# Two transformer blocks on one core: first projections among the transposes of h, and gate and up with 512 columns moving

## The reference

```python
# first block
h = rms_norm(x, mix_norm_g);  proj = h @ w_in          # queries, keys/values, gates, conv input
attn = nsa_attention(q, kv, gates, rel_bias, ...)      # compressed, selected and window branches
conv = silu(layer_norm(depthwise_conv31(a * sigmoid(g))))
x = x + concat([attn, conv]) @ w_out
h = rms_norm(x, ffn_norm_g)
u = depthwise_conv3(h @ w_up);  a, gate = split(u)      # 2 x 5632 columns
x = x + (silu(gate) * a) @ w_down;  x = rms_norm(x, final_norm_g)
# second block
ada = silu(c) @ w_ada + b_ada                           # six shift / scale / gate vectors
h = rms_norm(x, g_pre_mix) * (1 + scale_m) + shift_m;  z = h @ w_in_2
o = concat([mla_mixer(...), gla_mixer(...)]) @ w_out_2
x = x + gate_m * rms_norm(o, g_post_mix)
h = rms_norm(x, g_pre_ffn) * (1 + scale_f) + shift_f
f = (silu(h @ w_ffn_gate) * (h @ w_ffn_up)) @ w_ffn_down   # 5632 columns each
x = x + gate_f * rms_norm(f, g_post_ffn)
```

## Time and profile before

| what | value |
|---|---|
| runs | 2502.04, 2501.56, 2496.78 us; median 2501.56 |
| profiled execution | time 2500.57 us, span 2498.7 us |
| mean granted TensorE clock | 0.965 of full speed |
| busy share of the span | PE 94%, DVE 64%, ACT 44%, POOL 1% |
| HBM read | 494.31 MB |

### The profile page before, as it was taken

How to read it: one execution, slowest core, us unless ns; L and a number is a source line. 1 busy time by engine, 2 the same in 40 slices (tenths; PEclk the granted TensorE clock), 3 DMA queues, 4 the chain that set the end, 5 groups by cost and what they waited for, 6 DMA issues and landing times.

```text
span 2498.7 us, 37713 instructions
## 1 busy us (share of the span) xinstructions
PE 2359.4 (94%) x15624; PEld 2121.9 (85%) x15624; DVE 1603.2 (64%) x2266; ACT 1109.9 (44%) x1725; POOL 23.3 (1%) x59
## 2 busy tenths in 40 slices
PE   6989899899999999999979999996999999999997
PEld 5879777689998899998858787675999988999985
DVE  3996656678887778888765464646555555545444
ACT  3423566444444334444445464544434444444442
POOL 0000000000000000000000000000000000000000
PEclk9989989989999999999989899997999999999998
DMA  7745412668888888888854453252666667655552
GB/s 184 245 138 168 131 51 76 219 211 276 277 275 285 310 279 279 272 287 290 297 166 147 146 186 109 85 173 102 212 225 214 226 232 222 222 177 186 186 193 76
DMA packets 137770, 502.02 MB, mean 201 GB/s; under 512 B 15312, under 2 KB 15312, under 8 KB 137344
## 3 DMA queue, kind: packets, MB, share of 16 engines
q1 hardware_dynamic: 136368, 494.37, 58.6%
q0 software_dynamic: 1232, 5.24, 1.3%
HBM read 494.31 MB, written 5.24 MB: 200 GB/s over the span
## 4 chain that ended last, share of the span: by engine, by line
PE 84%; DVE 10%; ACT 3%; DMA 1%; issue 1%; POOL 1%; SPq 0%; ACTq 0%; DVEq 0%
PE bank L573 77%; DVE conv_y L1535 3%; DVE w_lo L1462 3%; PE bank L722 1%; DMA raw<-weights 1%; PE bank L757 1%; PE bank L545 1%; ACT w_hi L1034 1%; PE bank L610 0%; PE bank L739 0%; DVE wide L1480 0%; PE bank L622 0%; PE bank L752 0%; DVE x L1994 0%; DVE wide L1992 0%
## 5 line engine op out<-in xcount | busy, mean ns | idle before, releaser
L1462 DVE TENSOR_TENSOR w_lo<-raw,w_hi 128x1024 fp32r<-128x1024 f32 x737 | 888.0, 1220 | 550.6 <-ACT w_hi L1034 550.3
L573 PE MATMUL bank<-h_hi,w_hi 128*128 128x256 f32 x3472 | 993.7, 286 | 21.0 <-DVE w_lo L1462 20.6
L1034 ACT ACTIVATE w_hi<-raw 128x1024 fp32r<-128x1024 f32 x737 | 759.8, 1052 | 522.2 <-PE bank L573 503.4
L573 PE MATMUL bank<-h_lo,w_hi 128*128 128x256 f32 x3472 | 986.9, 284 | 0.0
L573 PE MATMUL bank<-h_hi,w_lo 128*128 128x256 f32 x3472 | 986.7, 284 | 0.0
L573 PEld LDWEIGHTS bank<-h_hi,w_hi 128*128 128x128 f32 x3472 | 670.1, 193 | 31.8 <-DVE w_lo L1462 30.9
L573 PEld LDWEIGHTS bank<-h_lo,w_hi 128*128 128x128 f32 x3472 | 670.4, 193 | 0.1
L573 PEld LDWEIGHTS bank<-h_hi,w_lo 128*128 128x128 f32 x3472 | 669.9, 193 | 0.0
L573 PE MATMUL bank<-w_hi,ff_hi 128*128 128x512 f32 x704 | 276.0, 392 | 2.9 <-DVE w_lo L1462 2.9
L573 PE MATMUL bank<-w_lo,ff_hi 128*128 128x512 f32 x704 | 274.0, 389 | 0.0
L573 PE MATMUL bank<-w_hi,ff_lo 128*128 128x512 f32 x704 | 274.0, 389 | 0.0
(11 more groups left out here) (293 smaller groups left out, 1818.1 us busy)
## 6 DMA issues: line engine op xcount, KB each, us to landing
raw<-weights SPq DMA_DIRECT2D x924, 512.0 KB, 4.4
bias_rows<-table POOLq DMA_DIRECT2D x1, 3072.0 KB, 35.5
raw<-weights SPq DMA_DIRECT2D x5, 504.0 KB, 3.4
x<-x SPq DMA_DIRECT2D x2, 1024.0 KB, 5.8
bias<-bias_rows POOLq DMA_DIRECT2D x1, 2048.0 KB, 17.1
out<-x SPq DMA_DIRECT2D x8, 256.0 KB, 2.0
lasting<-params SPq DMA_DIRECT2D x1, 550.0 KB, 7.7
raw<-weights SPq DMA_DIRECT2D x1, 488.0 KB, 3.2
```

The source lines that it names most:

```text
L573: t = e.matmul(out, s, m, start=opens and first and q == 0, stop=closes and last and q == 2)
L1034: e.activation(w_hi[:, n % PART_SLOTS, 0:widths[i]], raw[:, i % RAW_SLOTS, 0:widths[i]], ACT.Copy).then_inc(hi_ready, 1)
L1462: e.tensor_tensor(w_lo[:, slot, 0:widths[i]], raw[:, i % RAW_SLOTS, 0:widths[i]], w_hi[:, slot, 0:widths[i]].bitcast(F32), ALU.subtract).t ...
```

## The change

The first projections of a stage are issued among the transposes. `need(k)` turns up to four steps ahead, through four banks, and `project` calls it ahead of its wait for the weights. In stages 0 and 1 the first two tiles are made together (`tile_pair`), with their chunks laid out in turn; in stages 2 and 3 the first group runs so. ACT and DVE take weight chunks between their steps of h, at the steps in `WITH_H`, and DVE scales the second half of `wide` between them. The rel_bias table now comes before stage 0. In the second block's FFN gate and up are groups of 512 columns (the last of each half 256); the product has tokens on the partitions and is turned by PE in pairs of tiles (`turn_product`), after the first chunk of the next group. The ada chunks pause for the last of `out_attn` and the first pair of the first FFN, and then come at a rate of 0.6.

```diff
+FF_GROUPS = [[(6 * half + g, P * FF_HALF * half + 512 * g, min(512, P * FF_HALF - 512 * g)) for g in range(6)] for half in range(2)]
...
+    def project_pair(self, key, first, second, mat, cols, n):
+        self.groups[key] = [self.piece(mat, kt, col, n) for kt in range(KD) for col in cols]
+        self.pairs[first] = self.pairs[second] = key
...
+        if n == 3:
+            p.ada_until(2 * KD, 0)
...
+            p.project_pair("up_first", ("up_a", 0), ("up_g", 0), "w_up", (0, DFF), P)
+            p.ada_until(2 * KD, 0.6)
...
+        WITH_PAIR = {0: 0, 2: 1, 4: 2, 6: 3, 11: 4}
+        WITH_GROUP = {k: k // 2 for k in range(0, KD, 2)}
+        WITH_H = (WITH_PAIR, WITH_PAIR, WITH_GROUP, WITH_GROUP)
+        TURN_BANKS = ((6, 7, 0, 1), (6, 7, 0, 1), (6, 7, 4, 5), (6, 7, 4, 5))
...
+            def h_need(stage, freed):
+                turning = turn_steps(stage, freed)
+                done = [0]
+
+                def need(k):
+                    while done[0] < min(k + 4, KD):
+                        next(turning)
+                        done[0] += 1
+                    w.wait_ge(h_ready, 16 * stage + k + 1)
+
+                return need
+
+            def tile_pair(key, first, second, a_hi, a_lo, need, free_first, free_second):
+                both = (4, 5)
+                tiles["turn"] += 2
+                bank_of[first], bank_of[second] = both
+                whole(project(key, P, both, [banks[b][:, 0:T] for b in both], a_hi, a_lo, need, True, by_turns=True))
+                free[4], free[5] = free_first, free_second
...
+            need = h_need(0, lambda k: (h_ready, k + 1))
+            tile_pair("conv_first", ("conv_a", 0), ("conv_g", 0), h_hi, h_lo, need, (conv_a_ready, 1), (conv_g_ready, 1))
+            for j in range(1, CONV_TILES):
...
+            def turn_product(g):
+                for pair in ff_pairs(g):
+                    b = 6 + pair % 2
+                    fill(b)
+                    for at_tile in range(2):
+                        col = (2 * (pair - ff_pairs(g)[0]) + at_tile) * P
+                        for tt in range(TT):
+                            w.wait_ge(ffn_product, FF_TILES + 2 * g + tt + 1)
+                            t = e.transpose(banks[b][:, at_tile * T + tt * P:at_tile * T + (tt + 1) * P], product[:, tt, col:col + P], identity)
+                    t.then_inc(ff_turned, 1)
+                    free[b] = ff_ready, FF_TILES + pair + 1
...
+                for g, col, n in FF_GROUPS[half]:
+                    gating = group_steps(("gate", g), n, (0, 1), h_hi, h_lo, need)
+                    next(gating)
+                    if g % 6:
+                        turn_product(g - 1)
+                    whole(gating)
+                    free[0], free[1] = (ffn_silu, FF_TILES + 2 * g + 1), (ffn_silu, FF_TILES + 2 * g + 2)
+                    group(("up", g), n, (2, 3), h_hi, h_lo, need)
+                    free[2], free[3] = (ffn_product, FF_TILES + 2 * g + 1), (ffn_product, FF_TILES + 2 * g + 2)
...
+                    if k in WITH_H[stage]:
+                        round_until(FIRST_CHUNKS[stage] + WITH_H[stage][k])
...
+            def ff_round(g, first_chunk):
+                round_until(first_chunk + AHEAD)
+                for pair in ff_pairs(g):
+                    w.wait_ge(ff_turned, pair + 1)
+                    jj = 2 * (pair % 11)
+                    e.activation(ff_hi[:, jj:jj + 2, :].rearrange("p a t -> p (a t)"), banks[6 + pair % 2][:, :], ACT.Copy).then_inc(ff_rounded, 1)
+
             for half in range(2):
-                for j in range(FF_HALF * half, FF_HALF * (half + 1)):
-                    out = made(("gate", j))
-                    if j >= 2:
-                        w.wait_ge(ff_ready, FF_TILES + j - 1)
-                    e.activation(sw_g[:, j % 2, :], out[:, 0:T], ACT.Silu).then_inc(ffn_silu, 1)
-                    round_until(final["up", j] + AHEAD)
-                    w.wait_ge(ffn_product, FF_TILES + j + 1)
-                    e.activation(ff_hi[:, j % FF_HALF, :], sw_g[:, j % 2, :], ACT.Copy).then_inc(ff_rounded, 1)
+                for g, col, n in FF_GROUPS[half]:
+                    if g % 6:
+                        ff_round(g - 1, groups["gate", g][0][0])
+                    outs = made(("gate", g))
+                    if g:
+                        w.wait_ge(ff_turned, ff_pairs(g - 1)[-1] + 1)
+                    for tt in range(TT):
+                        e.activation(product[:, tt, 0:n], outs[tt][:, 0:n], ACT.Silu).then_inc(ffn_silu, 1)
...
+            def rest_h(stage, gain, factors, count):
+                scale_h(factors, count, (0, 1))
                 for k in range(KD):
+                    if k in (2, 6):
+                        scale_h(factors, count, (2 + k // 4,))
+                    if k in WITH_H[stage]:
+                        rests_until(FIRST_CHUNKS[stage] + WITH_H[stage][k])
...
+            def ff_rest(g, first_chunk):
+                rests_until(first_chunk + AHEAD)
+                for pair in ff_pairs(g):
+                    w.wait_ge(ff_rounded, FF_TILES + pair + 1)
+                    jj = 2 * (pair % 11)
+                    hi, lo = (which[:, jj:jj + 2, :].rearrange("p a t -> p (a t)") for which in (ff_hi, ff_lo))
+                    e.tensor_tensor(lo, banks[6 + pair % 2][:, :], hi.bitcast(F32), ALU.subtract).then_inc(ff_ready, 1)
 
             for half in range(2):
-                for j in range(FF_HALF * half, FF_HALF * (half + 1)):
-                    rests_until(final["gate", j] + AHEAD)
-                    out = made(("up", j))
-                    s, jj = j % 2, j % FF_HALF
-                    w.wait_ge(ffn_silu, FF_TILES + j + 1)
-                    e.tensor_tensor(sw_g[:, s, :], out[:, 0:T], sw_g[:, s, :], ALU.mult).then_inc(ffn_product, 1)
-                    w.wait_ge(ff_rounded, FF_TILES + j + 1)
-                    e.tensor_tensor(ff_lo[:, jj, :], sw_g[:, s, :], ff_hi[:, jj, :].bitcast(F32), ALU.subtract).then_inc(ff_ready, 1)
+                for g, col, n in FF_GROUPS[half]:
+                    if g % 6:
+                        ff_rest(g - 1, groups["gate", g][0][0])
+                    rests_until(final["gate", g] + AHEAD)
+                    outs = made(("up", g))
+                    for tt in range(TT):
+                        w.wait_ge(ffn_silu, FF_TILES + 2 * g + tt + 1)
+                        e.tensor_tensor(product[:, tt, 0:n], outs[tt][:, 0:n], product[:, tt, 0:n], ALU.mult).then_inc(ffn_product, 1)
```

More of the change, by code:

```diff
@@ L269, in __init__ @@
             self.final[key] = pieces[-1][0]
+        for key, pair in plan.pairs.items():
+            self.done[key], self.final[key] = self.done[pair], self.final[pair]
         self.sums = []
@@ L564, in project @@
                     hi, lo = part(i, w_hi, off, n), part(i, w_lo, off, n)
-                    first, last = at_piece == 0, at_piece == len(pieces) - 1
+                    span = len(outs) if by_turns else 1
+                    first, last = at_piece < span, at_piece >= len(pieces) - span
                     for o, out in enumerate(outs):
+                        if by_turns and o != at_piece % span:
+                            continue
                         if tile:
@@ L793, in tensor_program @@
                 free[pair[0]], free[pair[1]] = (residual, 8 + 2 * n + 1), (residual, 8 + 2 * n + 2)
[L795 to L796 removed]
+            need = h_need(1, lambda k: (h_ready, 16 + k + 1))
+            tile_pair("up_first", ("up_a", 0), ("up_g", 0), h_hi, h_lo, need, (ffn_a_conv, 1), (ffn_g_conv, 1))
             for half in range(2):
[L798 removed]
+                for j in range(FF_HALF * half or 1, FF_HALF * (half + 1)):
                     tile(("up_a", j), h_hi, h_lo, need, (ffn_a_conv, j + 1))
@@ L1014, in tensor_program @@
                     pair = (2 * (n % 2), 2 * (n % 2) + 1)
-                    group(("down2", half, n), 512, pair, ff_hi, ff_lo, ff_need)
+                    down = group_steps(("down2", half, n), 512, pair, ff_hi, ff_lo, ff_need)
+                    next(down)
+                    if n == 0:
+                        turn_product(6 * half + 5)
+                    whole(down)
                     if half:
```

93 lines of the change are left out of this document (47 added, 46 removed).

## The result

| | before | after |
|---|---|---|
| median | 2499.87 us (4 runs, 2496.78 to 2502.04) | 2436.67 us (4 runs, 2434.75 to 2437.06) |
| ratio | | 0.9747, 95% interval 0.973 to 0.9763 |
| span of the profiled execution | 2498.7 us | 2435.0 us |
| mean granted TensorE clock | 0.965 | 0.972 |

63.2 us faster by the medians and 63.7 by the spans, where 52 were forecast. The page after: the span, busy time, the granted clock in 40 slices, the chain by line, two groups, and two DMA issues.

What follows compares the result with a forecast made beforehand. The prediction saw a start waiting for DMA then DVE, four ramps where TensorE waits for the splitting of h, and a long TensorE-bound stretch; -14 - 22.6 - 15.3 = -51.9 us gave 2450 us, 8-in-10 range 2434 to 2470.

Steps and rivals of the forecast that it cites:

- The forecast's own band: Whole kernel: a new time of 2442 to 2458 us, chance 0.50.
- rival (e): Whole kernel: the start does better than 14 us, or the transposes hide; 2438 us, chance 0.10.
- Part 1: Start: the early table lets bias_rows go out at 13.5 us instead of 31.83, filling empty DMA time; -14 us.
- The first stage ... I add nothing: Ramp of the first stage: TensorE is earlier, but DMA and then DVE decide there, so no gain beyond part 1.
- the rule of the Trainium skill: Start: VectorE operations taking both SBUF ports block POOL's DMA descriptors; transfer up to 3.9 us later, term -10.
- Part 2: Ramps of stages 1 to 3: projections start among the transposes; gains 8.0, 5.7 and 8.9 us, term -22.6 us.
- 24 transposes, about 4 us: Ramps: transposes still to come among the matmuls, 0.13 us each warm to 0.22 at the low level, taken off the gain.
- rival (a): Ramps: the low clock outlasts them, +25 instead of -22.6, 2498 us; chance 0.03 in full, 0.12 in part (2462).
- The ada schedule: First FFN: the moved ada chunks are the same number and DVE has gaps, so nothing gained or lost.
- Part 3: Gate and up of the second block: 512 columns moving save 27 us, 88 transposes cost 11.7; term -15.3 us.
- (b): Gate and up: products late by 1.5 us for each of 12 groups, 2468 us; chance 0.09.
- (d): Gate and up: transpose breaks drop TensorE to 1.2 GHz, 30 us, together with (a) in full; 2528 us, chance 0.03.

Runs made afterwards that it cites:

- the five kernels with the same start: Five follow-up kernels with the same instructions as the kernel after up to the first attention scores, reached at 288.4 to 290.3 us.
- late_table: Kernel after, with the rel_bias matmul and the copy of its table put back behind stage 0; 2438.01 us, ratio 0.9758.
- early_table_only: Kernel before, with only the rel_bias matmul and table copy moved ahead of stage 0; 2489.89 us, ratio 0.9961.
- old_ada: Kernel after, with ada chunks at the rate of 0.58 throughout as before and no pause; 2446.38 us, ratio 0.9797.
- old_ada_steps: Kernel after, with the old ada rate and no pause, but stage 1 steps for taking weight chunks counting the ada chunks between; 2441.2 us, ratio 0.9779.
- no_cover: Kernel after, with each product turned right behind its up, without the next group's first chunk in between; 2451.15 us, ratio 0.9821.
- twice_turned: Kernel after, with every transpose of the product issued twice into the same place, 88 more; 2447.27 us, ratio 0.9786.
- turn_first: Kernel after, with all 32 transposes of a stage issued ahead of its first projection, still through four banks; 2443.42 us, ratio 0.979.
- two_banks: Kernel after, with h turned through two banks and two steps ahead instead of four and four; 2468.85 us, ratio 0.9876.
- bias_after_2: Kernel after, with bias_rows issued only when the second conv product is in conv_u; 2427.96 us, ratio 0.9721.

## Why the prediction was right, and where not

**Direction and range held; the forecast's own band (2442 to 2458) was missed by 5 us,** and the time came out at that of rival (e) (2438). Only a part of that is for the reasons (e) had named, a better start and cheaper transposes. The sum was 11.8 us short by the spans, and the largest pieces of this, 3.5 us ahead of stage 1 and 2.7 in the mixer behind its ramp, stood in no term.

**Part 1** (forecast 14, measured 14.7 at the scores, 16.3 to 18.2 by the five kernels with the same start). The number is right and two steps behind it are not. "The first stage ... I add nothing" failed: late_table shows 11.8 us from the interleaving alone. And the cause given, that the transfer must start early to fill empty time, holds only for the kernel before. With TensorE taking chunks from 18 us on the empty time was already half filled, the early transfer is worth 2.9 to 6.4 us, and it stood in the way of the weights for the second conv pair. The reasoning would have picked the wrong next step; bias_rows behind that pair is faster, clearly so when cut by rows. The landing took 35.5 us with three scale operations of DVE right behind the issue, and 35.5 without; the rule of the Trainium skill that the prediction weighed (SBUF — State Buffer, SBUF: two separate sides), by which the transfer would start up to 3.9 us late, is not borne out (those three operations take 1.8 us, so that is all that this comparison could have shown). early_table_only did give about that size (11.2 at the scores, 10.7 by the span), but its issue stood at 14.28 us and landed by 49.8, so not for that reason.

**Part 2** (8.0, 5.7, 8.9). The starts of the projections were forecast within 0.2 us of what the marks gave (2.8, 3.2, 3.5 us behind the first transposes, against 2.8, 3.4, 3.6). The term "24 transposes, about 4 us" was too large: among warm matmuls two of them cost 0.21 to 0.25 us (a step of six 512-wide matmuls takes 1.61 us and 6 x 0.2266 is 1.36), 2.5 to 3 us in all. Stage 1 gained 9.9, stage 2 7.0 (62.7 to 55.6 us). For stage 3, the 25.6 us from there to the end less the 15.7 of part 3 leaves 9.9. What the prediction didn't see is the split: most of stage 1 came without the interleaving, from the four banks and the other parts of the edit, which it listed as details. The low clock was over 3.2, 4.5 and 5.6 us after the first projection, as forecast ("within some 6 us"); rival (a) had no part.

**The ada schedule** ("the same number, DVE has gaps: nothing") is the step that failed outright, and in two places. In the pair, without the pause, 7.3 us are lost. The sums are indeed cheap, 0.6 us; but the steps in `WITH_PAIR` count all chunks, so with ada chunks between them w_hi is issued late. The other place is the last group of out_attn. In the kernel before, TensorE waits there for a weight rest, and the clock falls soon behind the wait (DVE's rests, the first matmul after the wait, then a stretch at 0.50):

```profile
479.44 2.36 DVE L1462 TENSOR_TENSOR w_lo<-raw,w_hi 128x1024 fp32r<-128x1024 f32 x2 [1.96 <-ACT w_hi L1034]
...
480.72 0.50 PE L573 MATMUL bank<-w_hi,mix_hi 128*128 128x512 f32 x1 [1.84 <-DVE w_lo L1462]
...
482.30:485.60 3.30, 3.30 (x9) 2.53 (x8) 3.30 (x4) 0.55 (x1) 0.00 (x0) 0.50 0.86 295
```

All four kernels with the old plan (before, early_table_only, old_ada, old_ada_steps) have this wait of 1.84 us some 13 us ahead of stage 1, and none of the ten with the pause has it. From the scores to stage 1 the four took 184.0 to 187.4 us and the ten 180.3 to 183.9. They differ in how long they ran at the low clock, 18.0 to 25.5 us and 14.7 to 23.5. With half of that time taken off (an estimate: one of 256 columns costs 0.213 us there and 0.121 at the high level) 174.7 to 175.0 and 172.1 to 173.0 are left. So the pause is worth about 2 us here by the wait and, by the same estimate, 1.7 for the low clock behind it. The cause looks like that in the pair: DVE had stood idle for 1.96 us until ACT's w_hi was there, so no ada sum was in its way, and `AHEAD`, by which ACT decides how far to round before it turns to the group's other work, counts the ada chunks too. That last link was read from the program and has no run of its own.

**Part 3** (forecast 27 - 11.7 = 15.3; measured 15.7). Both terms were too large and cancelled: two 256-wide matmuls take 0.2400 us and one of 512 0.2266, 25.7 us over 1920, and a transpose of the product 0.11, 9.7 us. The cover was judged rightly: just enough (1.2 us to spare), and 1.4 us a group if gone. Rivals (b) and (d) are settled by no_cover and twice_turned.

**The mixer** gained 2.7 us more than its ramp. After a pause the projections of gla_q ran at the low level from 1411.65 to 1420.9 before, and from 1376.2 to 1379.5 after, with the same instructions. The low stretches as a whole, before and after:

```profile
1407.30:1420.90 13.60, 10.44 (x24) 6.84 (x25) 6.29 (x22) 1.56 (x3) 0.00 (x0) 0.50 0.15 44
```

```profile
1372.70:1379.40 6.70, 4.25 (x11) 2.46 (x10) 3.19 (x17) 0.19 (x1) 0.00 (x0) 0.50 0.01 2
```

This goes with the ramp, 100 us ahead of it: the stretch is 13.6 us long in all four profiled executions with another ramp in stage 2 (before, early_table_only, turn_first, two_banks), and 6.8 in all ten with that of the kernel after. How one leads to the other no run here shows.

## What to carry to other kernels

A transfer that nobody needs for 200 us belongs where the weights in hand outlast it, not where the DMA engines happen to be idle in the old profile: an edit elsewhere may fill that hole first, and two edits that fill the same hole don't add. When several engines walk a hand-written table of steps, ask how far ahead each may run and what the steps count; in two of these runs split chunks taken too late cost 6.7 us and most of 19.5. Try the parts of a change apart: most of what stage 1 gained came without the interleaving that the change was made for.

## What the runs showed of the hardware

- Half the heads of bias_rows took 36.0 us, as long as all of them; half the rows of all heads took 18.1.
- Transposes alone preceded a rise of the clock: in turn_first the granted clock was 0.50 (1.2 GHz) from 478.0 to 478.5 us and 0.67 in the mean from 478.5 to 479.4, so it rose shortly before the first projection at 479.41 (it was 1.00 from 479.1 on). In stage 2 of the same run it stayed at 0.50 from 1273 to 1281.3, though TensorE was busy 7.31 of 8.3 us. The Trainium skill, TensorE: Matmul & The Clock Gate, Part 4: PE-mode transpose, says that the high level doesn't engage for transposes; stage 1 disagrees, stage 2 would fit.
- Equal work takes unequal time. From the first scores to stage 1 the ten kernels with the pause of the ada chunks give TensorE the same 892 instructions and the same waits, and the stretch took 180.3 to 183.9 us, with 14.7 to 23.5 us of it at the low clock. From stage 2 to stage 3, ten kernels with the same ramp took 386.6 to 395.7 us. What sets the level at each pause stays open; a difference of 3 us in the one stretch and 9 in the other needs no edit to explain it. Busy time, the same stretch in bias_after_2 and in the kernel after:

```profile
286.80:467.00 180.20, 175.02 (x892) 130.48 (x891) 116.67 (x249) 107.47 (x305) 1.23 (x3) 0.96 0.36 115
```

```profile
291.90:475.80 183.90, 178.73 (x892) 132.95 (x891) 116.71 (x249) 107.57 (x305) 1.22 (x3) 0.94 0.35 113
```
